# Five edits of order in the opening of a decoder kernel: weight requests ahead of bias reads, an exponential ahead of a weight split, a sum of squares inside a tile

## The reference, cut to what matters

```
qkv = h @ w_qkv                       # 1024 x 3072: 8 heads x (q, k, v), 128 columns each
q, k = rms_norm(q, q_gain), rms_norm(k, k_gain)     # per 64 channels
lam = exp(sum(lam_q1*lam_k1)) - exp(sum(lam_q2*lam_k2)) + lam_init
sc  = q_blk @ k^T * scale ; bias = rel_table[t5_bucket(pos_q - pos_k)]
a   = softmax(where(causal, sc + bias, -inf))
wts = a[first half] - lam * a[second half] ; o = wts @ v
```

## Time and profile before

| what | value |
|---|---|
| runs | 2266.74, 2272.76, 2274.61 us |
| profiled execution, first to last instruction (span) | 2264.9 us |
| TensorE busy | 2190.8 us, 97% |
| VectorE busy | 1257.8 us, 56% |
| ScalarE busy | 935.6 us, 41% |
| GpSimd busy | 821.9 us, 36% |
| granted TensorE clock, mean over the span | 0.994 |

### The profile page before, as it was taken

How to read it: one execution, slowest core, us unless ns; L and a number is a source line. 1 busy time by engine, 2 the same in 40 slices (tenths; PEclk the granted TensorE clock), 3 DMA queues, 4 the chain that set the end, 5 groups by cost and what they waited for, 6 DMA issues and landing times.

```text
span 2264.9 us, 25750 instructions
## 1 busy us (share of the span) xinstructions
PE 2190.8 (97%) x9948; PEld 1710.9 (76%) x9948; DVE 1257.8 (56%) x2181; ACT 935.6 (41%) x1536; POOL 821.9 (36%) x323
## 2 busy tenths in 40 slices
PE   5999999999999999999999999999998999999997
PEld 3677678888887667767888888887774588888886
DVE  4787675554247687773565552266957643333224
ACT  4567544333233476663333332232227632222223
POOL 2232344444444221113444444434330144444443
PEclk9999999999999999999999999999999999999999
DMA  7111233333222211112332332244310023333322
GB/s 267 56 56 56 75 105 93 100 96 108 90 95 86 71 39 47 33 38 75 95 101 93 103 104 92 98 128 158 120 48 28 29 94 102 93 99 105 100 88 84
DMA packets 58793, 200.99 MB, mean 89 GB/s; under 512 B 6608, under 2 KB 10208, under 8 KB 58672
## 3 DMA queue, kind: packets, MB, share of 16 engines
q1 hardware_dynamic: 55808, 194.94, 27.0%
q10 hardware_dynamic: 2864, 4.40, 0.6%
HBM read 197.19 MB, written 7.38 MB: 90 GB/s over the span
## 4 chain that ended last, share of the span: by engine, by line
PE 85%; DVE 9%; DMA 2%; ACT 2%; issue 1%; SPq 1%; POOL 0%; DVEq 0%; ACTq 0%
PE lin L506 24%; PE lin L507 23%; PE lin L508 23%; DVE arena L1615 3%; PE obank L818 2%; PE scores L796 1%; PE turn L622 1%; PE scores L800 1%; DVE arena L1559 1%; PE lin L540 1%; PE scores L656 1%; PE obank L699 1%; PE lin L541 1%; PE lin L542 1%; DMA a_bias_by_distance<-a_bias_rows 1%
## 5 line engine op out<-in xcount | busy, mean ns | idle before, releaser
L2377 POOL TENSOR_TENSOR w_lo<-slots,w_hi 128x1024 fp32r<-128x1024 f32 (+4 forms) x314 | 814.2, 2595 | 1419.1 <-ACT w_hi L1889 1408.1
L1889 ACT ACTIVATE w_hi<-slots 128x1024 fp32r<-128x1024 f32 (+4 forms) x314 | 349.2, 1112 | 626.6 <-DMA slots<-in_w_ffn_in 280.6
L506 PE MATMUL lin<-g_hi,w_hi 128*128 128x512 f32 x1408 | 553.3, 393 | 0.0
L508 PE MATMUL lin<-g_hi,w_lo 128*128 128x512 f32 x1408 | 548.7, 390 | 0.0
L507 PE MATMUL lin<-g_lo,w_hi 128*128 128x512 f32 x1408 | 548.6, 390 | 0.0
L506 PEld LDWEIGHTS lin<-g_hi,w_hi 128*128 128x128 f32 x1408 | 264.8, 188 | 63.8 <-issue 8.2
L507 PEld LDWEIGHTS lin<-g_lo,w_hi 128*128 128x128 f32 x1408 | 264.8, 188 | 55.8 <-issue 1.7
L508 PEld LDWEIGHTS lin<-g_hi,w_lo 128*128 128x128 f32 x1408 | 264.7, 188 | 55.4
L1160 DVE TENSOR_TENSOR h<-lin,h 128x512 f32<-128x512 f32 x72 | 49.7, 691 | 307.4 <-PE lin L508 298.2
L506 PE MATMUL lin<-f_hi,w_hi 128*128 128x512 f32 x528 | 205.4, 389 | 0.0
L507 PE MATMUL lin<-f_lo,w_hi 128*128 128x512 f32 x528 | 205.4, 389 | 0.0
(11 more groups left out here) (434 smaller groups left out, 3478.2 us busy)
## 6 DMA issues: line engine op xcount, KB each, us to landing
slots<-in_w_ffn_in SPq DMA_DIRECT2D x132, 512.0 KB, 3.5
slots<-in_w_ffn_out SPq DMA_DIRECT2D x48, 704.0 KB, 4.0
slots<-in_w_ple SPq DMA_DIRECT2D x24, 640.0 KB, 3.8
slots<-in_w_a_qkv SPq DMA_DIRECT2D x24, 512.0 KB, 3.5
slots<-in_w_c_in SPq DMA_DIRECT2D x23, 512.0 KB, 3.5
slots<-in_w_b_wo SPq DMA_DIRECT2D x16, 512.0 KB, 3.5
slots<-in_w_b_pair SPq DMA_DIRECT2D x8, 768.0 KB, 4.2
slots<-in_w_a_wo SPq DMA_DIRECT2D x16, 256.0 KB, 2.6
```

Of the source, the lines that this page charges most:

```text
L506: pe.matmul(bank[:, parity, :], hi, x_hi, start=k == 0, stop=False)
L508: mm = pe.matmul(bank[:, parity, :], lo, x_hi, start=False, stop=k == len(rhs) - 1)
L1889: ac.activation(w_hi[:, slot, at_], slots[:, slot, at_], ACT.Copy).then_inc(q.hi_made, 1)
L2377: po.tensor_tensor(w_lo[:, slot, at_], slots[:, slot, at_], w_hi[:, slot, at_].bitcast(F32), ALU.subtract).then_inc(q.weights_split, 1)
```

## The change

Five edits, all of order; no instruction is added or removed. On SyncE the request for weight group 3 goes ahead of the bands of parts 1 and 2, the request for group 4 ahead of the bias reads of part 1, and the request for group 5 ahead of those of part 2. On TensorE the first sum of squares moves from ahead of tile 2 into it, behind its second chunk. On ScalarE the exponential of lam moves ahead of `split(2)`, which is the high half of weight group 4.

```diff
@@ SyncE, loop over GROUPS
                 if name == "a_qkv" and k == 2:
                     a_bias_band(0)
                     a_bias_by_distance(0)
+                if name == "a_qkv" and k == 3:
                     a_bias_band(1)
                     a_bias_band(2)
-                if name == "a_qkv" and k == 3:
-                    a_bias_by_distance(1)
-                    a_bias_by_distance(2)
+                if name == "a_qkv" and k in (4, 5):
+                    a_bias_by_distance(k - 3)
@@ TensorE, a_step
-                def lin_(j):
+                def lin_(j, after=None):
...
-                        tile(TILE["a_qkv"] + 3 * s + j, (TILE["a_qkv"] + 3 * par + j) % 2, w, 0, gs)
+                        tile(TILE["a_qkv"] + 3 * s + j, (TILE["a_qkv"] + 3 * par + j) % 2, w, 0, gs, after=after)
...
                     pe.wait_ge(q.consts_in, 16)
-                    lin_(1); sums(0); lin_(2); sums(1)
+                    lin_(1); lin_(2, {1: lambda: sums(0)}); sums(1)
@@ ScalarE, a_step
                 if s == 0:
-                    squared(0); split(1); factor_(0); squared(1); factor_(1); split(2)
+                    squared(0); split(1); factor_(0); squared(1); factor_(1)
                     ac.wait_ge(q.lam_dots, 1)
                     ac.activation(lame, lamd, ACT.Exp).then_inc(q.lam_exps, 1)
+                    split(2)
```

## The result

| | before | changed |
|---|---|---|
| median of runs | 2273.66 us (4 runs, 2266.74 to 2274.61) | 2256.95 us (4 runs, 2255.96 to 2258.5) |
| ratio | | 0.9937, 95% interval 0.9921 to 0.9952 |
| span of the profiled execution | 2264.9 us | 2256.7 us |
| tile 5 starts | 68.71 us | 54.94 us |

The change makes the kernel 16.7 us faster by the medians. The two profiled executions are only 8.2 us apart, and the opening, up to tile 5, is 13.8 us shorter. The three numbers have to be brought together; that is the main question of the experiments.

A forecast was written before the change was run, and what follows sets the result against it. TensorE was taken as the bound, with only its opening stops, traced to late weight groups, to be won: 1.0 + 2.8 + 8.1 + 2.9 - 0.6 = 14.2 us, so 2272.76 - 14.2 = 2258.6; range 2252.5 to 2266.

The forecast's parts named there:

- Step 1: TensorE's opening: the first sum inside tile 2 fills the 0.83 us stop, so tile 2 ends sooner; gain 1.0 us.
- Step 2: Group 3 requested ahead of the bands lands at about 29, so the second sum no longer waits; gain 2.8 us.
- Step 3: Group 4 lands at 37.1, lam runs ahead of it; TensorE's stop before score(1) is 1.4 for 9.48 us; gain 8.1.
- Step 4: The shorter stop before score(1) does not lower TensorE's clock, so score(1) and tile 4 run faster; gain 2.9 us.
- Step 5: Group 5, behind part 1's reads, lands at 45.5 ahead of head 0's exponentials; cover half a microsecond, later waits cost 0.6.
- Its rival: Group 5 lands no sooner than 51.3, delaying head 0's exponentials; 4.9 us lost, gain 9.3, 2263.5 us; chance 0.23.
- The port lock: VectorE with two SBUF inputs and GpSimd block each other for a whole instruction; priced 0.1 to 0.2 us at L1348.
- The transfer of the gain to the median: The trace's gain carried over to the median run, 7.9 us above the traced span: 2272.76 - 14.2 = 2258.6.
- the prediction's own sign: Prediction is wrong if tile 5 starts at 54.5 and the last instruction is not some 14 us sooner.

The follow-up runs named there:

- undo_sum: The changed kernel with the first sum of squares put back ahead of tile 2; tile 5 starts at 55.53 us, for 54.94 in the change.
- requests_alone: The kernel before with SyncE's new request order alone; tile 5 starts at 55.61 us, for 68.71 before.
- undo_lam: The changed kernel with the exponential of lam put back behind the high half of group 4; tile 5 starts at 55.24 us.
- undo_requests: The changed kernel with SyncE's old request order put back, lam and the sum staying as changed; tile 5 starts at 64.06 us.
- lam_alone: The kernel before with only the exponential of lam moved ahead of the high half of group 4; tile 5 starts at 65.37 us.
- late_group5: The changed kernel with the request for group 5 put behind all eight bias reads; tile 5 starts at 62.90 us.
- all_early3: all_early2 with the angle moved back ahead of head 0's copies; tile 5 starts at 56.27 us, median 2256.44 us.
- all_early2: The change with lam's exponential and nlam earlier, tile 1 taken earlier, group 5 requested earlier, score(0) inside tile 3, angle later (output wrong); tile 5 at 52.24 us.

## Why the prediction was right

Forecast 2258.6 us, median measured 2256.95; tile 5 forecast at 54.5, measured 54.94. By its steps, the gain up to tile 5 (13.77) splits into 0.24 that the trace's tile 1 was early by itself, and:

- **Step 1, the sum inside tile 2**: 1.0 forecast, 1.09 by the trace (tile 2 starts 1.80 sooner, less 0.24, less 0.47 for the sum inside). As a gain of its own it failed: undo_sum reaches the second sum at the same time, and so do requests_alone and undo_lam, which differ in this edit alone. The step did not see that what it wins is lost again at the next wait.
- **Step 2, group 3**: 2.8 forecast, 1.81 measured (tile 3 at 37.38 for 40.52 is 3.14, less 1.09 and 0.24). The term was too large by the 0.95 us stop. Group 3 landed at 29.9, inside its cover of 30.8. What was missed is L1316, held by GpSimd's remainder of group 3, which the earlier group brought to that place (L1315 in the two later traces). In undo_sum, with the group 0.5 later, the hold falls on L1318, behind the take of tile 1 (1.91 us), and there is no stop.
- **Step 3, group 4 and lam**: 8.1 forecast, 7.99 measured. Group 4 landed at 37.2 (37.1 forecast), and lam ran at 38.84 (38.3). That the scores are the late one missed by a hair: where they alone decide (undo_requests, lam_alone), `biased(0)` comes 1.17 to 1.18 behind the start of `score(0)`, which here would be 44.09; it came at 44.17, when VectorE was through with its own lam arithmetic and the 1.31 us behind it. The step gave lam's place no price of its own, and undo_lam shows it has almost none once the group is early.
- **Step 4, the clock**: 2.9 forecast, 2.63 measured (9.16 us from `score(1)` to tile 4's end before, 6.53 after). The windows of 28 to 66 us, changed kernel and then before:

```profile
28.00:66.00 38.00, 35.41 (x159) 25.76 (x158) 28.60 (x64) 22.80 (x46) 11.75 (x5) 1.00 0.68 230
```

```profile
28.00:66.00 38.00, 24.92 (x96) 17.84 (x96) 19.41 (x42) 12.80 (x23) 9.69 (x5) 0.87 0.58 198
```

- **Step 5, group 5**: 0.6 forecast as a cost, 0.0 measured. It reached ScalarE at 46.12 (landing 45.5 forecast), and the traces with group 5 at 46.7 and later have tile 5 later: the cover was all but used up, as the step said. Its rival, that part is given back behind group 5, priced a landing at 51.3 at 4.9 us; late_group5 had 8.0. That price was too low, because the first turn is late as well and the stops bring the low clock back.

The port lock was put in as a sentence against the change with 0.1 to 0.2 us on L1348. There it cost 0.08 us, since L1348, 2.23 us for the 0.16 that it takes in undo_requests, let VectorE come to `biased(0)` that much behind the scores. It cost the stop of 0.95 us at L1316, a place that nobody had looked at. The Trainium skill, "SBUF — State Buffer" (its part on the two separate sides), says that the lock goes to whichever starts first, for the whole instruction, and concerns VectorE in a two-port mode or with two SBUF inputs; the traces agree in that each long instruction began behind a remainder (L1316 with two inputs, 0.19 us behind, 2.79 long; L1319 of all_early3 with one, 0.08 behind, 2.61 long). That the one with a single input was in a two-port mode is not shown by the trace.

The transfer of the gain to the median held, but the text had no ground for it. It carried a local gain over to a median although the profiled execution of before was the shortest of its four, and took it that the rest of the span stays as it is. By the prediction's own sign (tile 5 at 54.5 and the last instruction not some 14 us sooner) the first pair of traces says that it is wrong: the last instruction came 8.2 us sooner. The sign was bad and not the gain, since two traces of the kernel before differ by 10.0 us in the same rest. The medians say 16.7; both differences carry a few us of clock. That 2258.6 came within 1.7 us of the measured median is in part luck, with single runs spread by 3.3 and the difference at 12.6 to 16.7 by the occasion; tile 5, within 0.44 us, is the stronger confirmation, and even there the 1.0 too much of step 2 is mostly made good by the 0.6 that step 5 counted in vain and by 0.24 of tile 1 that no edit brought.

## What to carry to other kernels

When one queue serves weights and other reads, look first at which consumer's engine stands still, and then for what stands ahead of its request; here 13.1 of 13.8 us came from three requests and at most 0.7 from moving the arithmetic that seemed to wait. Edits that cure the same stop must be priced together, since each alone looks worth 3 to 13 us and the second one adds 0.3 to 0.5. When an edit moves a transfer, look at what the engines that it feeds will then run beside: here an earlier weight group brought a GpSimd instruction beside a VectorE instruction on the path. Measure an effect of 0.5% by a local time in the trace, such as the start of a fixed tile, and keep the rest of the span apart.

## What the runs showed of the hardware that was not expected

- The granted clock of this single core falls to 0.50 for 3.4 to 14.1 us at a time, in or behind stops of TensorE and in all 14 traces at the very end, and which stops draw it differs between executions of one program: later than 90 us it was 18.0 and 42.6 us in two traces of the kernel before, with 10.0 us between the rests of the span. The length of the stop alone does not tell: 2.77 us drew no low clock in the first trace of before, 2.03 us drew it in all_early3.
- A narrow VectorE instruction can cost ten times its own time beside GpSimd: 0.22 us became 2.41 (64 columns), 0.16 became 2.23 (one column). Which instruction it hits can turn on less than 0.1 us: L1319 began together with the remainder in all_early2 and took 0.42, and 0.08 behind it in all_early3 and took 2.61.
